# Grouped-query attention of a macaron encoder: head pairs between query tiles and out-projection units, on one core

## Chip, core and metric

The kernel runs on one core of a Trainium2 chip. The metric is the device time in microseconds of one execution. It is measured several times and the median counts.

## What is computed

The reference prepends 16 meta tokens to 256 frames (272 tokens, width 1024) and runs two layers. Each layer is a half-step SwiGLU block (hidden width 2816), a token mixer and another half-step SwiGLU block, each with an RMS norm before and after. The mixer of the first layer is stick-breaking attention, that of the second, which the change touches, is grouped-query attention with 16 heads of 64, four key and value heads, a window of two chunks of 64 frames, the 16 meta tokens always visible, rotary positions and a learned sink logit for each head:

```python
s_meta = einsum('bnqhgd,bmhd->bnhgqm', qf, k_meta) * scale
s_band = where(visible, einsum('bnqhgd,bnkhd->bnhgqk', qf, k_band) * scale, -inf)
p = softmax(concatenate([s_meta, s_band, sink], axis=-1), axis=-1)
o_frames = einsum(p_meta, v_meta) + einsum(p_band, v_band)
return o @ w_out
```

All is fp32. The meta rows of the output are dropped at the end, so in the last two sub-layers only frames are needed, except for the keys and values of the meta tokens.

## The kernel before

**Products.** Activations lie transposed, features on partitions and tokens in columns. Every weight product is made of three fp32r products, because weights and activations are each split into a high part (rounded to fp32r) and a low part: w_lo·y_hi + w_hi·y_hi + w_hi·y_lo (`three`, lines 1049 to 1054). Small products (scores, values, rotations, transposes, sums over partitions) are plain fp32, and the profile shows two records for each of them, except for a transpose, which has one.

**Weights.** They come in panels of 128 x 2048 (1 MB), numbered through all six sub-layers. SyncE loads them in this order into two raw slots (line 376), each load waiting for the low split two panels earlier. ScalarE casts a half of a panel into w_hi (`hi_half`, 427 to 435, cast at 435), VectorE subtracts for w_lo (`lo_half`, 661 to 667). There are four slots of w_hi and w_lo, and a slot is free when TensorE has signalled `panel_done` for the panel four earlier. An input panel has 256 output columns in two tiles of 128 (each 8 x 3 products), an output panel takes 256 input rows (8 output tiles x 2 x 3 products).

**The sub-layers** (`plan`, 117 to 124) are ffn, sb (stick-breaking), ffn, ffn, swa (grouped-query), ffn. On TensorE each begins with a head: the first three input panels are worked at the same time, k by k, at the pace in which VectorE and ScalarE deliver the normed input (1062 to 1105). Lines 1413 to 1431 are the sums of squares for the post-norm and four idle products that fill the wait for it. In sb the attention is written in head pairs and issued between its own input tiles and output columns by a written-out order of slots (`SB_AT`, `SB_HI`, `SB_LO`, lines 1248 to 1272); the two heads of a pair alternate on the two halves of TensorE's rows (scores, 1170 to 1181) or columns (values, 1221 to 1235).

**The swa sub-layer before.** Panels come in the order K, Q0 to Q3, V (`SWA_PANELS`). TensorE finishes all six (`in_panel`, 1107), with the rotations for rope (`rotate`, 1127, line 1136) between the last ones, and VectorE drains each panel with the norm's factor (line 768) and applies rope (`rope`, 752: sine product 756, sum 760; the cosine product is GpSimd's, line 410). ScalarE copies the keys into kd for both halves of the partitions (568), GpSimd copies the value windows (420).
Then comes the attention, head by head, in steps `st` (1335 to 1343): `scores(st)`, `turn(st - 8)`, `values(st - 9)`. Around it VectorE does `mask_scores` (scale and mask, line 880), `maxima` over two heads at a time (889), `sink_maxima` for four (899 to 903), `normalise` (910 to 918) and `save_o` (923); ScalarE does `exps(st - 5)` (575 to 580), the copy of the turned probabilities (593) and the high part of the output (584). Weight splits stand still in these steps. At the end TensorE does the four output panels (`out_panel`, 1390), the first of them waiting for all outputs.

## Time and profile before

| | |
|---|---|
| runs: median (lowest to highest) | 1082.48 us (1080.39 to 1085.07), 3 runs |
| the profiled execution's own time | 1080.6 us |
| its span, first to last instruction | 1078.8 us |
| TensorE busy | 1058.6 us, 98% |
| VectorE busy | 636.9 us, 59% |
| ScalarE busy | 508.8 us, 47% |
| mean granted TensorE clock | 0.995 |

Engines are called PE (TensorE), PEld (its weight loads, which overlap it), DVE (VectorE), ACT (ScalarE), POOL (GpSimd) and SP (SyncE). PEclk is the granted TensorE clock as a share of 2.4 GHz. A timeline row has the start, the length from the first start to the last end, the engine, the line, the names written and read, the shape, and how many records it merges; in brackets is the idle time in front of it and who ended it. Since products are pipelined, the end of one row lies behind the start of the next, and prices are best read from start to start.

### The profile page before, as it was taken

To read this page: it belongs to the slowest core of one execution; us is meant where nothing else is said; L and a number is where in the kernel's file an instruction comes from. 1 tells how busy PE (TensorE), PEld (TensorE's weight loads), DVE (VectorE), ACT (ScalarE), POOL (GpSimd) and SP (SyncE) were. 2 spreads that over 40 slices of the span, in tenths; PEclk is the share of its full clock that TensorE was granted. 3 is DMA by queue.
4 is the path that set the end of the run, shared out by engine and by line. 5 is a ranking of instruction groups with operands and counts; after the bars stand their busy time and mean duration, and the time that the engine had idled before them with its cause. 6 is when DMAs were issued, how large, how long until landed. Compare 5 with 4: busy or idle time off the path is not lost.

```text
span 1078.8 us, 19938 instructions
## 1 busy us (share of the span) xinstructions
PE 1058.6 (98%) x8082; PEld 1019.0 (94%) x8082; DVE 636.9 (59%) x840; ACT 508.8 (47%) x710; POOL 11.5 (1%) x20
## 2 busy tenths in 40 slices
PE   9999999999999999999999999999997999999997
PEld 8999999999899999999999999999995799999986
DVE  5765544576564776554457755534777667656443
ACT  5643433456454564343345543433544746544433
POOL 0000000000000000000000000000021000000000
PEclk9999999999999999999999999999998999999999
DMA  7564555413433265544542645545250053655551
GB/s 273 201 228 166 183 163 189 156 45 114 149 124 116 84 228 199 173 176 168 184 156 101 233 173 171 180 165 186 78 188 8 7 190 123 252 180 185 196 176 39
DMA packets 25828, 170.13 MB, mean 158 GB/s; under 512 B 3120, under 2 KB 3888, under 8 KB 5808
## 3 DMA queue, kind: packets, MB, share of 16 engines
q1 hardware_dynamic: 24624, 167.26, 43.9%
q10 hardware_dynamic: 1152, 2.11, 0.6%
q8 instruction: 41, 0.67, 0.2%
q14 instruction: 11, 0.09, 0.0%
HBM read 168.31 MB, written 1.05 MB: 157 GB/s over the span
## 4 chain that ended last, share of the span: by engine, by line
PE 93%; DVE 3%; ACT 1%; DMA 1%; issue 0%; SPq 0%; DVEq 0%; ACTq 0%
PE ps L1052 24%; PE ps L1053 24%; PE ps L1054 24%; PE ps L1087 3%; PE ps L1096 3%; PE ps L1089 3%; PE ps L1352 2%; PE ps L1353 2%; PE ps L1351 2%; PE ps L1211 1%; PE ps L1313 1%; DMA raw<-in_panels_dram 1%; PE ps L1299 1%; PE ps L1230 1%; PE ps L1423 1%; PE ps L1178 1%
## 5 line engine op out<-in xcount | busy, mean ns | idle before, releaser
L435 ACT CAST w_hi<-raw 128x1024 fp32r<-128x1024 f32 x310 | 310.2, 1048 | 404.2 <-PE ps L1054 313.1
L666 DVE TENSOR_TENSOR w_lo<-raw,w_hi 128x1024 fp32r<-128x1024 f32 x310 | 368.8, 1229 | 197.5 <-ACT w_hi L435 197.1
L1052 PE MATMUL ps<-y_hi,w_lo 128*128 128x272 f32 (+1 forms) x1522 | 440.1, 289 | 1.8 <-DVE y_lo L923 1.0
L1054 PE MATMUL ps<-y_lo,w_hi 128*128 128x272 f32 (+1 forms) x1522 | 437.3, 287 | 0.0
L1053 PE MATMUL ps<-y_hi,w_hi 128*128 128x272 f32 (+1 forms) x1522 | 435.6, 286 | 0.0
L1052 PEld LDWEIGHTS ps<-y_hi,w_lo 128*128 128x128 f32 x1522 | 286.7, 188 | 3.8 <-issue 2.9
L1053 PEld LDWEIGHTS ps<-y_hi,w_hi 128*128 128x128 f32 x1522 | 286.7, 188 | 0.3
L1054 PEld LDWEIGHTS ps<-y_lo,w_hi 128*128 128x128 f32 x1522 | 286.7, 188 | 0.0
L1053 PE MATMUL ps<-h_hi,w_hi 128*128 (+1 forms) x528 | 152.5, 289 | 0.0
L1054 PE MATMUL ps<-h_lo,w_hi 128*128 (+1 forms) x528 | 151.9, 288 | 0.0
L1052 PE MATMUL ps<-h_hi,w_lo 128*128 (+1 forms) x528 | 151.5, 287 | 0.0
L1054 PEld LDWEIGHTS ps<-h_lo,w_hi 128*128 128x128 f32 x528 | 99.5, 189 | 0.0
L1052 PEld LDWEIGHTS ps<-h_hi,w_lo 128*128 128x128 f32 x528 | 99.5, 188 | 0.0
L1053 PEld LDWEIGHTS ps<-h_hi,w_hi 128*128 128x128 f32 x528 | 99.4, 188 | 0.0
L741 DVE TENSOR_TENSOR hid<-act,ps 128x544 f32<-128x544 f32 (+1 forms) x44 | 31.2, 710 | 73.7 <-PE ps L1054 73.7
L736 DVE TENSOR_TENSOR act<-ps,rms_inv 128x544 f32<-128x544 f32 (+1 forms) x44 | 31.5, 716 | 58.8 <-PE ps L1054 55.1
L1087 PE MATMUL ps<-y_hi,w_lo 128*128 128x272 f32 (+1 forms) x238 | 61.7, 291 | 3.6 <-DVE y_hi L1036 2.7
L1089 PE MATMUL ps<-y_hi,w_hi 128*128 128x272 f32 (+1 forms) x238 | 60.8, 287 | 0.0
L1087 PEld LDWEIGHTS ps<-y_hi,w_lo 128*128 128x128 f32 x238 | 44.7, 188 | 6.2 <-DVE y_hi L1036 4.8
L1089 PEld LDWEIGHTS ps<-y_hi,w_hi 128*128 128x128 f32 x238 | 44.8, 188 | 0.0
L1096 PE MATMUL ps<-y_lo,w_hi 128*128 128x272 f32 (+1 forms) x238 | 36.5, 287 | 0.0
L1352 PE MATMUL ps<-w_hi,h_hi 128*128 128x512 f32 x88 | 34.8, 395 | 0.0
(134 smaller groups left out, 926.6 us busy)
## 6 DMA issues: line engine op xcount, KB each, us to landing
raw<-in_panels_dram SPq DMA_DIRECT2D x155, 1024.0 KB, 4.8
raw<-in_panels_dram SPq DMA_DIRECT2D x6, 256.0 KB, 8.8
sq<-in_panels_dram SPq DMA_DIRECT2D x1, 1024.0 KB, 10.0
out_dram<-fT SPq DMA_DIRECT2D x4, 256.0 KB, 2.0
const<-in_const_dram ACTq DMA_DIRECT2D x1, 920.0 KB, 4.7
xT<-in_x_dram ACTq DMA_DIRECT2D x3, 272.0 KB, 8.0
raw<-in_panels_dram SPq DMA_DIRECT2D x4, 128.0 KB, 3.8
gain_row<-in_row_dram SPq DMA_DIRECT2D x1, 512.0 KB, 5.5
```

What stands on the lines that cost most here:

```text
L435: nc.scalar.copy(w_hi[:, g % SLOTS, part], raw_part(g, part)).then_inc(hi_ready, 1)
L666: nc.vector.tensor_tensor(w_lo[:, g % SLOTS, part], raw_part(g, part), w_hi[:, g % SLOTS, part].bitcast(F32), ALU.subtract).then_inc(lo_re ...
L736: nc.vector.tensor_tensor(act[:, j % 2, :, t0:L], ps[:, b0:b0 + 2, t0:L], spread(rms_inv, 2, t0), ALU.mult).then_inc(gate_ready, 1)
L741: nc.vector.tensor_tensor(hid[:, j % 2, :, t0:L], act[:, j % 2, :, t0:L], ps[:, b0:b0 + 2, t0:L], ALU.mult).then_inc(h_ready, 1)
L1052: nc.tensor.matmul(dst, w_lo[:, slot, pc], yh, start=first, stop=False)
L1053: nc.tensor.matmul(dst, w_hi[:, slot, pc], yh, start=False, stop=False)
L1054: return nc.tensor.matmul(dst, w_hi[:, slot, pc], yl, start=False, stop=last)
L1087: nc.tensor.matmul(dst, w_lo[:, g % SLOTS, pc], y_hi[:, k, t0:L], start=(k == 0), stop=False)
L1089: nc.tensor.matmul(dst, w_hi[:, g % SLOTS, pc], y_hi[:, k, t0:L], start=False, stop=False)
L1096: nc.tensor.matmul(ps[:, BANK_IN[i][c], t0:L], w_hi[:, g % SLOTS, pc], y_lo[:, k, t0:L], start=False, stop=False)
L1351: nc.tensor.matmul(dst, hh[:, cols], w_lo[:, slot, at:at + 512], start=first, stop=False)
L1352: nc.tensor.matmul(dst, hh[:, cols], w_hi[:, slot, at:at + 512], start=False, stop=False)
```

## The change

The panels come as K, V, Q0 to Q3. The head works K, V and Q0; the other six query tiles are issued one in each slot, at 256 columns. The attention runs in head pairs, twelve slots in all, with the 16 units of the out-projection (12 products each) from slot 6 on. Weight splits are spread over the slots by halves. The key copy kd becomes kx, the keys with the two partition halves exchanged. Mask, scale and maximum become one operation, `tensor_tensor_reduce`, which writes s = -(score*scale + mask), since op is `(in0 + in1) * scale` with scale -1/8 and the mask is 0 or -1e30, and the running minimum that starts at minus the sink. Exponentials and normalisation go by pairs. The outputs have buffers of their own (sw_hi, sw_lo). The core of the diff:

```diff
-SWA_PANELS = [4, 0, 1, 2, 3, 5]
-SW_EXP, SW_LAG = 5, 8
+SWA_PANELS = [4, 5, 0, 1, 2, 3]
+SW_K, SW_V, SW_Q = 0, 2, 4
+SW_TILES, SW_SLOTS = 6, 12
+SW_HI = [1] * 10 + [2, 2, 2]
+SW_LO = [2] + [1] * 9 + [2, 2, 3]
+SW_OUT = [(6, 0), (6, 1), (7, 0), (7, 1), (5, 0), (5, 1), (0, 0), (1, 0)]
+SW_FILL = {6: ([(0, 0)], [(0, 1)]), 7: ([(0, 2)], []), 8: ([(1, 0)], [(1, 1)]), 9: ([(1, 2)], [(0, 3)]),
+           10: ([(1, 3)], [(2, 0)]), 11: ([(2, 1)], [(2, 2), (2, 3)])}
```

ScalarE's order:

```diff
+                    for st in range(SW_SLOTS + 1):
+                        if 0 <= st - 4 < PAIRS:
+                            save_p(st - 4)
+                        hi_halves(2 + sum(SW_HI[:st]), SW_HI[st])
...
+                        if 0 <= st - 2 < PAIRS:
+                            exps(st - 2)
+                        if 0 <= st - 4 < PAIRS:
+                            o_high(st - 4)
```

VectorE's new operation and its order:

```diff
+                    def logits(p):
+                        for half in range(2):
+                            h = 2 * p + half
+                            v.wait_ge(s_done, p + 1)
+                            if p >= 3:
+                                v.wait_ge(pt_done, 2 * (p - 3) + half + 1)
                             for c in range(2):
                                 k0, k1 = SW_COL[c], SW_COL[c] + SW_KEYS[c]
+                                nc.vector.tensor_tensor_reduce(
+                                    out=s[:, p % 3, half, k0:k1], in0=ps[:, half, k0:k1], in1=cst("mask_sw", P, k0, k1),
+                                    scale=-SCALE, scalar=neg_sinks[:, h:h + 1], op0=ALU.add, op1=ALU.min,
+                                    accum_out=neg[:, p % 3, half, c:c + 1]).then_inc(neg_ready, 1)
...
+                    for st in range(SW_SLOTS + 1):
+                        n0 = sum(SW_LO[:st])
+                        if 0 <= st - 3 < PAIRS:
+                            normalise(st - 3)
+                        lo_halves(n0, 1)
+                        if st < SW_TILES:
+                            drain_tile(st)
+                        if st == 0:
+                            rope(0)
+                            rope(1)
+                        elif st in (2, 4, 6):
+                            rope(st // 2 + 1)
+                        if 0 <= st - 1 < PAIRS:
+                            logits(st - 1)
+                        if 0 <= st - 4 < PAIRS:
+                            o_low(st - 4)
+                        lo_halves(n0 + 1, SW_LO[st] - 1)
```

TensorE's blocks and their order:

```diff
+                    def scores(p):
+                        kv = p // 2
+                        pe.wait_ge(roped, 2 + p // 2)
+                        if p == 0:
+                            pe.wait_ge(kx_ready, 2)
+                        if p >= 1:
+                            pe.wait_ge(neg_ready, 4 * p)
+                        for at, tok, n in SW_RUNS:
+                            q0 = META if at == 0 else META + P
+                            for half in range(2):
+                                r = slice(HD * half, HD * half + HD)
+                                keys = qkv[r, SW_K + kv // 2] if half == kv % 2 else kx[r, kv // 2]
+                                mm = nc.tensor.matmul(ps[:, half, at:at + n], qkv[r, SW_Q + p, q0:q0 + P],
+                                                      keys[:, tok:tok + n], start=True, stop=True,
+                                                      skip_group_check=True)
                         mm.then_inc(s_done, 1)
...
+                    def values(p):
+                        vc = slice(HD * (p // 2), HD * (p // 2) + HD)
+                        pe.wait_ge(pt_saved, 2 * p + 2)
+                        if p >= 1:
+                            pe.wait_ge(ol_ready, 8 + p)
                         for n, (c, _, zero) in enumerate(SW_WIN):
+                            for half in range(2):
+                                r = slice(HD * half, HD * half + HD)
+                                mm = nc.tensor.matmul(ps[r, 4, P * c:P * c + P], vt[:, n, vc],
+                                                      p_t[:, p % 2, half, P * n:P * n + P], start=(zero == 0),
+                                                      stop=(zero > 0), skip_group_check=True)
+                        mm.then_inc(sw_o, 1)
...
+                    def out_unit(j, n):
+                        g = t.g_out + j
+                        pe.wait_ge(lo_ready, 2 * g + 2)
+                        pe.wait_ge(ol_ready, 8 + 2 * j + 2)
...
+                    for st in range(SW_SLOTS):
+                        if st < SW_TILES:
+                            in_tile(st)
+                        for unit in SW_FILL.get(st, ([], []))[0]:
+                            out_unit(*unit)
+                        if st == 0:
+                            rotate(0)
+                            rotate(1)
+                        elif st in (2, 4, 6):
+                            rotate(st // 2 + 1)
+                        if 0 <= st - 1 < PAIRS:
+                            scores(st - 1)
+                        if st == 1:
+                            turn_v()
+                        if 0 <= st - 4 < PAIRS:
+                            values(st - 4)
+                        for unit in SW_FILL.get(st, ([], []))[1]:
+                            out_unit(*unit)
+                        if 0 <= st - 3 < PAIRS:
+                            turn(st - 3)
+                    for n in range(4):
+                        out_unit(3, n)
```

GpSimd keeps its five cosine products, now into two alternating buffers (rot_c), and does the value windows (two fills and five copies) after the second one. PSUM banks: scores 0 and 1, turned probabilities 2 and 3, outputs of a pair 4, rotations 5, tiles 6 and 7; the first out units take 6, 7, 5 and at last 0 and 1 in half banks (SW_OUT).

## Rows read from the trace of the kernel before

**Rows 1.** The page, busy time by engine (share of the span, instructions)

```profile
PE 1058.6 (98%) x8082; PEld 1019.0 (94%) x8082; DVE 636.9 (59%) x840; ACT 508.8 (47%) x710; POOL 11.5 (1%) x20
```

**Rows 2.** Windows: stretch, busy by engine, PEclk, DMA share, GB/s

```profile
240.00:340.00 100.00, 99.07 (x802) 91.40 (x801) 60.54 (x81) 52.79 (x64) 0.00 (x0) 1.00 0.33 117
818.40:828.60 10.20, 7.75 (x33) 5.40 (x31) 8.52 (x27) 5.41 (x21) 1.34 (x1) 0.50 0.00 1
```

**Rows 3.** Timeline of TensorE in the grouped-query sub-layer: start us, length us, what

```profile
794.62 1.16 PE L1136 MATMUL ps<-qkv,const 128*128 128x272 f32 x4 [1.32 <-DVE qkv L768]
...
803.30 0.49 PE L1052 MATMUL ps<-y_hi,w_lo 128*128 128x272 f32 x1
...
809.55 1.99 PE L1136 MATMUL ps<-qkv,const 128*128 128x272 f32 x8
811.47 3.28 PE L1284 MATMUL ps<-kd,qkv 64*128 64x144 f32 x28
...
817.86 1.38 PE L1326 MATMUL ps<-const,v_win 128*128 128x128 f32 x8 [3.11 <-DVE rot_s L756]
...
823.17 1.12 PE L1299 MATMUL ps<-const,s 128*128 128x128 f32 x4 [2.45 <-DVE s L918]
...
831.05 0.86 PE L1284 MATMUL ps<-kd,qkv 64*128 64x144 f32 x4
831.84 0.65 PE L1299 MATMUL ps<-const,s 128*128 128x128 f32 x4
832.42 1.09 PE L1313 MATMUL ps<-p_t,vt 128*64 128x128 f32 x8
833.44 0.86 PE L1284 MATMUL ps<-kd,qkv 64*128 64x144 f32 x4
...
858.21 0.35 PE L1052 MATMUL ps<-y_hi,w_lo 128*128 128x256 f32 x1 [1.01 <-DVE y_lo L923]
...
880.84 1.74 PE L1423 MATMUL ps<-sq,const 128*128 128x256 f32 x6
```

**Rows 4.** Timeline of TensorE in the stick-breaking attention

```profile
275.21 1.14 PE L1230 MATMUL ps<-fT,v_tok 128*64 128x272 f32 x12 [0.93 <-ACT fT L525]
276.28 0.41 PE L1203 MATMUL ps<-sp,const 128*128 128x32 f32 x2
...
289.38 1.20 PE L1178 MATMUL ps<-qkv 64*128 64x16 f32 x12
290.51 0.39 PE L1052 MATMUL ps<-y_hi,w_lo 128*128 128x272 f32 x1
...
293.73 1.20 PE L1178 MATMUL ps<-qkv 64*128 64x16 f32 x12
```

**Rows 5.** Timeline of VectorE, the grouped-query sub-layer

```profile
781.37 2.36 DVE L666 TENSOR_TENSOR w_lo<-raw,w_hi 128x1024 fp32r<-128x1024 f32 x2
...
812.45 1.39 DVE L880 SCALAR_TENSOR_TENSOR s<-ps,const 128x352 f32<-128x352 f32 x3 [1.91 <-PE ps L1284]
813.75 0.94 DVE L889 TENSOR_REDUCE top<-s 128x2 f32<-128x288 f32 x2
...
820.23 0.71 DVE L756 TENSOR_TENSOR rot_s<-ps,const 128x544 f32<-128x544 f32 x1
...
821.74 0.52 DVE L880 SCALAR_TENSOR_TENSOR s<-ps,const 128x352 f32<-128x352 f32 x1
...
822.58 0.98 DVE L918 TENSOR_SCALAR s<-s,inv 128x144 f32<-128x144 f32 x4
```

**Rows 6.** Timeline of ScalarE, the same stretch

```profile
834.93 0.58 ACT L593 COPY p_t<-ps 128x512 f32<-128x512 f32 x1 [0.70 <-PE ps L1299]
...
836.17 0.19 ACT L578 ACTIVATION_READ_ACCUMULATOR s<-s,neg 128x1 f32 x1
...
857.50 3.90 ACT L435 CAST w_hi<-raw 128x1024 fp32r<-128x1024 f32 x4
```

**Rows 7.** The page, DMA issues: KB each, median us to landing

```profile
raw<-in_panels_dram SPq DMA_DIRECT2D x155, 1024.0 KB, 4.8
```

More of the change, by code:

```diff
@@ L139, in bank_post, with out_tile, out_pair, first_col @@
     return bank_out(t)[2]
-ROT_BANK = [4, 6, 4, 6, 4]
-ROPE_AT = {4: 3, 6: 4}
+def out_tile(ps, t, d):
+    if t.kind == "swa":
+        bank, half = SW_OUT[d]
+        return ps[:, bank, 256 * half:256 * half + 256]
+    return ps[:, bank_out(t)[d], t.t_out:L]
+def out_pair(ps, t, n):
+    if t.kind == "swa" and n < 3:
+        return ps[:, SW_OUT[2 * n][0], :].rearrange("p (a n) -> p a n", a=2)
+    if t.kind == "swa":
+        return ps[:, 0:2, 0:256]
+    b0 = bank_out(t)[2 * n]
+    return ps[:, b0:b0 + 2, t.t_out:L]
+def first_col(t, i):
+    return META if t.kind == "swa" and i >= 2 else t.t_in
 HEAD = 3
@@ L339, in build @@
         pairs_before = [11 * sum(1 for t in SUBS[:u] if t.kind == "ffn") for u in range(7)]
-        drained_before = [sum(t.n_in for t in SUBS[:u] if t.kind == "swa") for u in range(7)]
         def steps(eng, n, body):
@@ new lines, in rope @@
+                    def rope(b):
+                        c0 = 0 if b == 0 else META
+                        row = SW_K if b == 0 else SW_Q + 2 * b - 2
+                        turned = ps[:, 0:2, 0:L] if b == 0 else ps[:, 5, :].rearrange("p (a n) -> p a n", a=2)
+                        v.wait_ge(rot_done, b + 1)
+                        nc.vector.tensor_tensor(rot_s[:, :, c0:L], turned, spread(cst("sin"), 2, c0),
+                                                ALU.mult).then_inc(rs_ready, 1)
+                        v.wait_ge(rs_ready, b + 1)
+                        v.wait_ge(rc_ready, b + 1)
+                        nc.vector.tensor_tensor(qkv[:, row:row + 2, c0:L], rot_s[:, :, c0:L],
+                                                rot_c[:, b % 2, :, c0:L], ALU.add).then_inc(roped, 1)
+                        v.wait_ge(roped, b + 1)
@@ new lines, in o_low @@
+                    def o_low(p):
+                        v.wait_ge(oh_ready, 8 + p + 1)
+                        nc.vector.tensor_tensor(sw_lo[:, p, :], ps[:, 4, 0:SEQ], sw_hi[:, p, :].bitcast(F32),
+                                                ALU.subtract).then_inc(ol_ready, 1)
+                    for i in range(3):
+                        drain_head(i)
+                    v.wait_ge(sinks_landed, 16)
+                    nc.vector.tensor_scalar(neg_sinks[:], sinks[:], -1.0, None, ALU.mult).then_inc(sinks_ready, 1)
@@ L1048, in _, with three @@
         def _(pe):
-            def three(dst, slot, col, yh, yl, first, last):
+            def three(dst, slot, col, yh, yl, first, last, shared=False):
                 pc = slice(col, col + P)
-                nc.tensor.matmul(dst, w_lo[:, slot, pc], yh, start=first, stop=False)
-                nc.tensor.matmul(dst, w_hi[:, slot, pc], yh, start=False, stop=False)
-                return nc.tensor.matmul(dst, w_hi[:, slot, pc], yl, start=False, stop=last)
+                nc.tensor.matmul(dst, w_lo[:, slot, pc], yh, start=first, stop=False, skip_group_check=shared)
+                nc.tensor.matmul(dst, w_hi[:, slot, pc], yh, start=False, stop=False, skip_group_check=shared)
+                return nc.tensor.matmul(dst, w_hi[:, slot, pc], yl, start=False, stop=last, skip_group_check=shared)
             for t in SUBS:
@@ new lines, in turn @@
+                    def turn(p):
+                        for half in range(2):
+                            h = 2 * p + half
+                            pe.wait_ge(p_ready, 2 * h + 2)
+                            if p == 0:
+                                pe.wait_ge(v_saved_a, half + 1)
+                            else:
+                                pe.wait_ge(pt_saved, h - 1)
+                            for n, (c, k0, _) in enumerate(SW_WIN):
+                                at = SW_COL[c] + k0
+                                mm = nc.tensor.transpose(ps[:, 2 + half, P * n:P * n + P],
+                                                         s[:, p % 3, half, at:at + P], cst("ident"))
+                            mm.then_inc(pt_done, 1)
```

413 lines of the change are left out of this document (160 added, 253 removed).

## Prediction

> **What bounds the kernel now.** I read the page first: TensorE is busy for 98% of the span, VectorE for 59% and ScalarE for 47% [rows 1]. So only TensorE's own work, its few idle stretches and its clock are worth anything. The windows show where the clock fails: the whole stick-breaking attention runs at granted clock 1.00, but 818.4 to 828.6 us, the front of the grouped-query attention, at 0.50 [rows 2], the lower of the two levels (1.2 instead of 2.4 GHz), with 7.75 us of 10.2 busy. TensorE had just been idle for 3.11 us there.
>
> TensorE's timeline from 793 to 881 us [rows 3] shows the rest. The first query panel ends at 794.62 − 1.32 = 793.30; a panel takes 809.55 − 803.30 = 6.25 us, so the stretch that the change rewrites begins at 787.05 (the end of the head that is paced by the norm) and ends at 880.84, where the post-norm sums begin: **93.8 us**. In it TensorE is idle for 1.32 (VectorE drains late, between weight splits), 3.11 (the value transposes wait for a rope), 2.45 (first probabilities) and 1.01 us (last output's low part): 7.9 us. In the steady part one head costs 831.84 − 831.05 = 0.79 for scores, 0.58 for four transposes, 833.44 − 832.42 = 1.02 for values.
>
> **The change, part by part, on TensorE.** All prices are start to start.
>
> - Query tiles. Four query panels take only the 256 frame columns, no longer 272. The out-projection has that width: (880.84 − 858.21) / 192 products = 0.1179 us each [rows 3]. Six tiles of 24 products are left (the third head panel lies before 787.05): 16.98 us. A tile between blocks of another kind pays for the change-over: one at 272 columns took 293.73 − 290.51 = 3.22 us [rows 4], times 256/272 = 3.03. I take 6 × 3.03 = 18.2. The head's third panel saves 48 × 0.0074 = 0.35 before 787.05 (0.0074 is 16/256 of 0.1179).
> - Rotations. Four full products in 811.47 − 809.55 = 1.92 [rows 3]: 0.48 each. Two of 272 and eight of 256 columns: 4.6.
> - Scores. Now both heads of a pair are issued turn about, on the two halves of the array's rows. Rows 3 have this by accident: seven heads in a row, odd and even, took 3.28 us, 0.94 a pair, against 2 × 0.79. The stick-breaking scores, already written in pairs, took 290.51 − 289.38 = 1.13 for 432 columns [rows 4]; for 352, 0.92. I take 0.96: 8 × 0.96 = 7.7.
> - Transposes: as before, 64 of them, 16 × 0.58 = 9.3. Value transposes once, 1.3 (8 of them, 1.38 long [rows 3]).
> - Values. A pair's products alternate between two halves of the array's columns. The stick-breaking values do just that: 276.28 − 275.21 = 1.07 for a pair with 544 columns each [rows 4], where the same columns one after the other would take twice that by the pace of rows 3 (512 columns in 1.02). With 512: 1.01, I take 1.02: 8.2, where 16 × 1.02 = 16.3 were.
> - Out-projection: 192 products at 0.1179 = 22.6, as before, but 12 of 16 units now stand between attention blocks. With about ten change-overs at (3.22 − 24 × 0.1179 × 272/256) = 0.21 at most, I take 1.8: 24.4.
>
> Sum: 18.2 + 4.6 + 7.7 + 9.3 + 1.3 + 8.2 + 24.4 = **73.7**, so 93.8 − 73.7 = 20.1, plus 0.35 is 20.4 us. The old 7.9 us of idling and the slow stretch are within the 93.8 and so within this gain, if nothing takes their place. A page speaks against the interleaving: TensorEngine Tiling (Array Packing) in the Trainium skill, section "Key Properties", says that a change of tiling mode drains the array. The trace prices this at no more than the 0.21 above; and the pairs halve the number of changes inside attention.
>
> **Do the other engines keep up?** One slot of TensorE, in the middle (tile 3.03, rotation 0.9 in every second, scores 0.96, values 1.02, transposes 1.17): 7.1 or 6.2 us. From slot 6 on units (1.6) take the tile's place; slot 7 is the shortest: 4.75.
> - VectorE [rows 5]: normalising a pair 1.4 (from 0.43 after 821.74 to 822.58 + 0.98), one weight split 1.18 (2.36 for two), a tile's drain about 0.4 (rope's 0.71 is for twice the width), rope 1.5 in every second slot (820.23 to 821.74), o_low 0.4, and the logits. Without the logits 4.9 or 3.4.
> - The new logits operation is in no row. Four a pair, of 144 and 208 columns. Below: no dearer than the plain one it resembles, 0.43 for 352 columns (three in 1.30), so 1.0 a pair with four starts. Above: as dear as the old operation and the old maximum one after the other, 2 × 0.43 + 0.94 = 1.8 a pair. It is one pass like the first, so I take 1.3. That makes 6.2 or 4.7 us on VectorE against 7.1 or 6.2: hidden. In slot 7 it is 4.7 against 4.75.
> - ScalarE [rows 6]: a save and one head's exponentials 836.36 − 834.93 = 1.43, twice, one conversion 0.98 (3.90 for four), o_high and the sinks 0.6: 4.4 us. Hidden. kx is two copies in slot 0, where twelve copies for kd were.
> - GpSimd: five cosine products as before, and seven copies and fills in the place of six. All its work in the kernel is 11.5 us [rows 1]; the part that the value transposes need, two products and the copies, is about half of that and starts at 787, so it ends by 793, before slot 1 asks at 795.7. rot_c now alternates between two buffers, so rope waits for it less.
> - DMA: SP's loads are in the same order; each waits for the split two panels earlier and lands 4.8 us later [rows 7]. Splits now come one half a slot, so loads spread over the attention, where rows 2 show the queue idle. Only the first output panel comes late (by the walk its load starts at about 795, ScalarE could cast it at 797) and holds the first exponentials back to about 803, and the first normalisation starts there anyway.
>
> Walking the slots with these prices, three places are tight. The first out unit (slot 6) follows o_low of pair 1 by 0.4 us; unit (1,0) in slot 8 meets o_low of pair 3 with nothing to spare; and where a scores block follows a logits group the semaphore hop counts. I give these 1.2 us together: below, 0; above, with logits at 1.8 a pair, about 3, since o_low stands behind the logits on VectorE. The last panel's units follow the last o_low by 1.7 us, and ScalarE has two conversions (1.95) left when they start, released by the third panel's end as now, so the post-norm is as before.
>
> Net: 20.4 − 1.2 = **19.2 us**. The profiled execution took 1080.6 us, so 1061.4; the median of the runs is 1.9 above it, so 1063.3. I forecast 1063 us, with TensorE at granted clock 1.00 through the stage, since the denser stick-breaking stage shows that for the same mix [rows 2].
>
> **Rivals.**
> - A: chained slots. VectorE and ScalarE serve tiles, ropes, logits, outputs and splits in one fixed order, so one late operation delays a drain, a load, then a tile. The widths above are for average slots; if 1 us is lost in six of the eight middle slots, 6 of 19 us are given back: 1069. For: slot 7 has no margin. Against: in most slots VectorE has 1 to 1.5 us to spare. Chance 0.13.
> - A2: the logits operation streams at half the pace of the old one: 4 × 0.43 = 1.7 a pair, with four starts 2.1 [rows 5]. That is 0.8 more in each slot; most of it is absorbed where VectorE waits for the scores anyway, but o_low is pushed past the first out units, 2 to 4 us lost: 1066. Chance 0.03. A page would have it so: the Vector Engine (DVE) Microarchitecture Reference in the Trainium skill, section "Points that are easy to get wrong", says that an operation of this accumulating family with two non-bf16 SBUF sources has half throughput. Here one source lies in PSUM, and no run so far shows it.
> - B: pairs do not overlap, as with two heads' values one after the other. Then scores cost 8 × 0.64 and values 8 × 1.02 more, 13.3: 1076.5. Against: rows 4 have both shapes. 0.05.
> - C, slower: the new logits operation is far dearer. Then VectorE sets the slot: slots 1 to 8 would take 4.2 + 4t each (t for one operation), the rest 27 us, which equals 93.8 at t = 1.04, against 0.3 taken. Already at t = 1.4 it is 8 × 9.8 + 27 = 105.4, 11.6 us more than now: 1094. Against: the old maximum, a reduction too, took 0.94 for a pair's 704 columns [rows 5]. 0.03.
> - D: only a third of the gain arrives, by A and B together: 1078 to 1085. 0.03.
>
> **Numbers.** The forecast itself has 0.73 (A 0.13, A2 0.03, B 0.05, C 0.03, D 0.03). What a measurement of this kernel can tell from no change is about 0.5%, 5.4 us. Faster 0.94, same 0.03, slower 0.03. Range: below, no new waits and no change-over cost, 1.2 + 3 less, 1059; above, A's 1069 and a margin for the runs' own scatter (1080.4 to 1085.1), 1070.
>
> **What would show it.** TensorE from the end of the head to the post-norm sums: about 75 us. Scores of a pair below 1.1 and values below 1.1. No idle of more than 0.5 us, least of all before the value transposes. No clock at 0.50 in the stage. Logits: 16 × 2 operations of about 0.3 us and a reading of the accumulator, if it has a record of its own. If the idle on TensorE behind VectorE adds up to over 3 us, A is right. If a pair takes the sum of two heads, B. The forecast is wrong above 1070.

## Result, and the profile after

| | before | after |
|---|---|---|
| median (lowest to highest), 4 executions each | 1082.67 us (1080.39 to 1085.07) | 1056.49 us (1056.02 to 1056.70) |
| the profiled execution's own time / span | 1080.6 / 1078.8 us | 1056.58 / 1054.8 us |
| mean granted clock of that execution | 0.995 | 0.999 |

The ratio is 0.9768, 95% interval 0.9754 to 0.9782: 2.3% faster. Between the two profiled executions the difference is 24.0 us, between the medians 26.2. The forecast, 1063 us with a range from 1059 to 1070, had the sign and the mechanism and gave too little: 19.2 us of gain in the profile where 24.0 came, and a range that ends 2.5 us above the measured time.

The page of the changed kernel, the two lines that answer to [rows 1] and the span:

```profile
span 1054.8 us, 20040 instructions
...
PE 1042.6 (99%) x8114; PEld 1007.8 (96%) x8114; DVE 629.9 (60%) x864; ACT 508.1 (48%) x712; POOL 10.9 (1%) x21
```

TensorE is now idle for 12 us in all, before for 20. The window over the rewritten stretch (stretch, busy PE, PEld, DVE, ACT, POOL, PEclk, DMA share, GB/s) answers to [rows 2]:

```profile
786.00:857.00 71.00, 70.91 (x658) 64.78 (x656) 58.01 (x161) 50.25 (x133) 9.47 (x12) 1.00 0.36 129
```

TensorE is busy for 70.91 of 71.00 us and the clock is at 1.00 throughout: nothing is left of the 0.50 stretch. TensorE's timeline, to be set against [rows 3] (L1281 and L1284 rotations, L1301 scores, L1339 value transposes, L1316 transposes, L1328 values, L1059 the first product of a tile or unit, L1462 the post-norm sums):

```profile
789.10 1.08 PE L1281 MATMUL ps<-qkv,const 128*128 128x272 f32 x4
...
794.77 1.09 PE L1339 MATMUL ps<-const,v_win 128*128 128x128 f32 x8
795.62 0.36 PE L1059 MATMUL ps<-y_hi,w_lo 128*128 128x256 f32 x1
...
798.54 1.02 PE L1284 MATMUL ps<-qkv,const 128*128 128x256 f32 x4
799.50 0.39 PE L1301 MATMUL ps<-qkv 64*128 64x144 f32 x1
...
800.49 0.39 PE L1059 MATMUL ps<-y_hi,w_lo 128*128 128x256 f32 x1
...
810.21 1.09 PE L1328 MATMUL ps<-p_t,vt 128*64 128x128 f32 x16
811.23 1.09 PE L1316 MATMUL ps<-const,s 128*128 128x128 f32 x8
812.08 0.36 PE L1059 MATMUL ps<-y_hi,w_lo 128*128 128x256 f32 x1
...
817.08 1.09 PE L1316 MATMUL ps<-const,s 128*128 128x128 f32 x8
818.12 0.35 PE L1059 MATMUL ps<-sw_hi,w_lo 128*128 128x256 f32 x1
...
824.11 1.04 PE L1316 MATMUL ps<-const,s 128*128 128x128 f32 x8
824.90 0.36 PE L1059 MATMUL ps<-sw_hi,w_lo 128*128 128x256 f32 x1
...
828.51 1.09 PE L1316 MATMUL ps<-const,s 128*128 128x128 f32 x8
829.69 0.36 PE L1059 MATMUL ps<-sw_hi,w_lo 128*128 128x256 f32 x1
...
856.68 1.74 PE L1462 MATMUL ps<-sq,const 128*128 128x256 f32 x6
```

One slot can be read in it: the tile from 795.62, the rotation 0.96 from 798.54, a pair's scores 0.99 from 799.50, the next tile from 800.49. A pair's values take 811.23 − 810.21 = 1.02 and its eight transposes 812.08 − 811.23 = 0.85, or 0.79 at 824.11, where a unit stands ahead of them instead of the values; a weight product follows in both cases. They are longer only where TensorE waits behind them: 1.04 at 817.08, in front of unit (0,0), and 1.18 at 828.51, in front of unit (1,0). These are two of the three places that the forecast called tight; the third, scores behind a logits group, shows no wait.

VectorE (the new operation is L907, its accumulator has a record of its own):

```profile
796.11 0.36 DVE L907 CUSTOM_DVE_ANT_0 s<-ps,const,neg_sinks 128x144 f32<-128x144 f32 x1
796.40 0.08 DVE L907 DVE_READ_ACCUMULATOR2_ANT neg<- 128x1 f32 x1
796.40 0.43 DVE L907 CUSTOM_DVE_ANT_0 s<-ps,const,neg_sinks 128x208 f32<-128x208 f32 x1
...
797.40 0.08 DVE L907 DVE_READ_ACCUMULATOR2_ANT neg<- 128x1 f32 x1
...
827.60 0.37 DVE L907 CUSTOM_DVE_ANT_0 s<-ps,const,neg_sinks 128x144 f32<-128x144 f32 x1 [1.33 <-PE ps L1301]
...
829.12 0.42 DVE L928 TENSOR_TENSOR sw_lo<-ps,sw_hi 128x256 fp32r<-128x256 f32 x1
```

From 796.11 to 797.40 the four operations of a pair take 1.29 us, as taken in the sum (1.3). In slot 7 the scores come late for VectorE (it waits 1.33), so o_low of pair 3 starts at 829.12, and unit (1,0) starts 0.57 later.

### The profile page after: what moved, and what is told of

It reads as the page before. It is cut to its first block, busy times and chain, and to the rows that moved or that the text cites. A ratio compares the mean times of both kernels' runs of the same rounds, so it can differ in the third digit from the quotient of the medians.

```text
span 1054.8 us, 20040 instructions
## 1 busy us (share of the span) xinstructions
PE 1042.6 (99%) x8114; PEld 1007.8 (96%) x8114; DVE 629.9 (60%) x864; ACT 508.1 (48%) x712; POOL 10.9 (1%) x21
## 4 chain that ended last, share of the span: by engine, by line
PE 95%; DVE 1%; DMA 1%; ACT 1%; issue 0%; SPq 0%; DVEq 0%; ACTq 0%
PE ps L1059 25%; PE ps L1060 25%; PE ps L1061 25%; PE ps L1095 3%; PE ps L1104 3%; PE ps L1097 3%; PE ps L1395 2%; PE ps L1396 2%; PE ps L1394 2%; PE ps L1197 1%; DMA raw<-in_panels_dram 1%; PE ps L1216 1%; PE ps L1462 1%; PE ps L1328 1%; PE ps L1301 1%; PE ps L1164 1%
## 5 line engine op out<-in xcount | busy, mean ns | idle before, releaser
L1059 PE MATMUL ps<-y_hi,w_lo 128*128 128x272 f32 (+1 forms) x1458 | 421.7, 289 | 0.8 <-DVE pre_ms L722 0.6
L1061 PE MATMUL ps<-y_lo,w_hi 128*128 128x272 f32 (+1 forms) x1458 | 418.9, 287 | 0.0
L1060 PE MATMUL ps<-y_hi,w_hi 128*128 128x272 f32 (+1 forms) x1458 | 417.4, 286 | 0.0
L1059 PEld LDWEIGHTS ps<-y_hi,w_lo 128*128 128x128 f32 x1458 | 274.7, 188 | 2.7 <-issue 1.9
L1060 PEld LDWEIGHTS ps<-y_hi,w_hi 128*128 128x128 f32 x1458 | 274.6, 188 | 0.2
L1061 PEld LDWEIGHTS ps<-y_lo,w_hi 128*128 128x128 f32 x1458 | 274.7, 188 | 0.0
L1059 PE MATMUL ps<-h_hi,w_lo 128*128 (+1 forms) x528 | 151.5, 287 | 0.0
L1059 PEld LDWEIGHTS ps<-h_hi,w_lo 128*128 128x128 f32 x528 | 99.5, 188 | 0.0
L1095 PE MATMUL ps<-y_hi,w_lo 128*128 128x272 f32 (+1 forms) x238 | 61.5, 290 | 3.8 <-DVE y_hi L1043 2.7
L1097 PE MATMUL ps<-y_hi,w_hi 128*128 128x272 f32 (+1 forms) x238 | 60.6, 286 | 0.0
L1095 PEld LDWEIGHTS ps<-y_hi,w_lo 128*128 128x128 f32 x238 | 44.8, 188 | 6.3 <-DVE y_hi L1043 4.8
L1097 PEld LDWEIGHTS ps<-y_hi,w_hi 128*128 128x128 f32 x238 | 44.8, 188 | 0.0
L1104 PE MATMUL ps<-y_lo,w_hi 128*128 128x272 f32 (+1 forms) x238 | 36.5, 287 | 0.0
```

What stands on the lines that cost most here:

```text
L1059: nc.tensor.matmul(dst, w_lo[:, slot, pc], yh, start=first, stop=False, skip_group_check=shared)
L1060: nc.tensor.matmul(dst, w_hi[:, slot, pc], yh, start=False, stop=False, skip_group_check=shared)
L1061: return nc.tensor.matmul(dst, w_hi[:, slot, pc], yl, start=False, stop=last, skip_group_check=shared)
L1095: nc.tensor.matmul(dst, w_lo[:, g % SLOTS, pc], y_hi[:, k, c0:L], start=(k == 0), stop=False)
L1097: nc.tensor.matmul(dst, w_hi[:, g % SLOTS, pc], y_hi[:, k, c0:L], start=False, stop=False)
L1104: nc.tensor.matmul(ps[:, BANK_IN[i][c], c0:L], w_hi[:, g % SLOTS, pc], y_lo[:, k, c0:L], start=False, stop=False)
```

## Experiments

Eleven runs were made: nine variants, and each of the two kernels once more. Those of one group ran on one chip, beside the kernel before; its median there was 1080.57 us (28 executions) for the first four, 1080.12 (9) for the next four, 1081.78 (9) for the last three. The changed kernel itself ran first and in the last group (1056.49 and 1056.92), so differences of the middle ones from it are good to about half a microsecond.

### Why the old kernel scatters: the clock

The first kernel is the kernel before, unchanged.

> The kernel before, once more, to see why its executions scatter by 4.7 us (1080.4 to 1085.1) where those of the changed kernel scatter by 0.7. Theory (clock): each execution loses more or less to a lowered granted clock in the attention, so the longer executions show a lower mean clock; 0.995 goes with about 1080.5, and 1085 should go with about 0.990. Rival (memory or start-up): the mean clock is the same, 0.995, in long and short executions, and the extra time lies outside the attention.

Its twelve executions, each with its mean granted clock, and those of the kernel before that ran beside it:

| mean clock | e0, us | before, same chip, us |
|---|---|---|
| 0.993 to 0.997 | 1079.38, 1079.65, 1080.53, 1080.92 | 1078.76 to 1082.18 (19) |
| 0.991 | 1081.94 to 1082.96 (6) | 1082.11 to 1082.86 (6) |
| 0.989 | 1084.59, 1085.47 | 1084.02, 1084.33, 1084.59 |

The clock theory holds: with one exception (1082.18 at 0.995) the clock alone sorts all 40 executions into these three groups of times. A mean of 0.991 over 1080 us is some 19 us at half clock by estimate, where the profiled execution has 10.2 in the attention and a little at the very end.

The second kernel gives TensorE something to do in the two idle stretches:

```diff
+                    def fill(bank, count):
+                        for _ in range(count):
+                            nc.tensor.matmul(ps[:, bank, 0:160], cst("ones"), cst("sin", P, 0, 160),
+                                             start=True, stop=True, skip_group_check=True)
                     def turn_v():
+                        pe.wait_ge(s_ready, 4)
+                        fill(3, 9)
                         pe.wait_ge(win_ready, 4)
...
+                        if st == SW_LAG:
+                            pe.wait_ge(rs_ready, 5)
+                            fill(5, 7)
                         if 0 <= st - SW_LAG < NH:
                             turn(st - SW_LAG)
```

> The kernel before with sixteen small fp32 products more, whose results are not used, issued into its two idle stretches (nine ahead of the value transposes, seven ahead of the first probabilities). Theory (clock): the granted clock stays at 1.00 through the attention; the 5.4 us after the second stretch that ran at the lower level shrink by 2.7, the idling itself stays: 1078 to 1080 us, and the executions scatter by less than 1.5 us. Rival (the clock has another cause than the idling): the 0.50 stretch stays and the time is 1082 to 1084, with the old scatter.

Measured: 1077.53 us, 1077.18 to 1078.23 in eleven executions, every one at 0.999 or 1.000. Its timeline (L1320 are the fillers), and the window over the attention:

```profile
814.34 2.71 PE L1320 MATMUL ps<-const 128*128 128x160 f32 x18 [0.42 <-DVE s L880]
...
820.16 2.17 PE L1320 MATMUL ps<-const 128*128 128x160 f32 x14 [1.27 <-DVE rot_s L756]
```

```profile
811.00:855.00 44.00, 40.80 (x297) 32.12 (x294) 32.30 (x104) 27.23 (x95) 2.67 (x3) 1.00 0.00 1
```

Most of the two idle stretches is now filled with work of no use: what is left of them is 0.42 us ahead of the first fillers and 1.27 ahead of the second. The attention ran at 1.00 and the time fell by 3.0 us against the median beside it, to half a microsecond below the range that was expected, and by more against the executions at 0.991. The scatter went from 6 us to 1. So the idling, not the attention's kind of work, brings the clock down, and the loss differs from one execution to the next. The clock did not fall behind the short stretches that are left in any execution. Why the low level lasts once 10 us and once 20 stays open.

### Pairs without interleaving

The kernel before with TensorE's order changed alone:

```diff
-                    for st in range(NH + SW_LAG + 1):
-                        if st < NH:
-                            scores(st)
+                    for st in range(0, NH + SW_LAG + 2, 2):
+                        for h in (st, st + 1):
+                            if h < NH:
+                                scores(h)
                         if st == 6:
                             turn_v()
-                        if 0 <= st - SW_LAG < NH:
-                            turn(st - SW_LAG)
-                        if st - SW_LAG >= 1:
-                            values(st - SW_LAG - 1)
+                        if st - SW_LAG >= 2:
+                            values_pair((st - SW_LAG) // 2 - 1)
+                        for h in (st - SW_LAG, st - SW_LAG + 1):
+                            if 0 <= h < NH:
+                                turn(h)
```

values_pair alternates between the halves as the changed kernel does.

> The kernel before, with TensorE alone reordered: scores, values and transposes by head pairs, values alternating between the halves, nothing put in between and the other engines' orders as they were. Theory (the pairs save work, the interleaving hides the chain): TensorE's work falls by about 17 us, but VectorE's 3.6 and ScalarE's 3.1 us a pair now exceed TensorE's 2.8, so only 6 to 10 us arrive: 1073 to 1077, with idle TensorE behind VectorE or ScalarE at each pair. Rival (the pairs alone are the gain): 1064 to 1067.

Measured: 1077.08 us (1075.96 to 1077.87), 3.5 us less than the kernel before beside it, where 6 to 10 were expected. TensorE's busy time falls by 10 us, from 1058.6 to 1048.2, and its idle time grows by 7, from 20 to 28. What is new in it is the wait of the values for ScalarE's copies of the turned probabilities, 8.5 us in seven waits. Four rows of TensorE's timeline (L1299 transposes, L1345 values, L1284 scores) and two of ScalarE's (L578 an exponential, L593 the copy):

```profile
832.59 1.09 PE L1299 MATMUL ps<-const,s 128*128 128x128 f32 x8
833.61 0.87 PE L1284 MATMUL ps<-kd,qkv 64*128 64x144 f32 x8
...
839.04 1.09 PE L1345 MATMUL ps<-p_t,vt 128*64 128x128 f32 x16 [1.56 <-ACT p_t L593]
...
842.73 1.09 PE L1345 MATMUL ps<-p_t,vt 128*64 128x128 f32 x16 [1.57 <-ACT p_t L593]
```

```profile
841.24 0.42 ACT L578 ACTIVATE s<-s,neg 128x144 f32<-128x144 f32 x1
...
842.10 0.57 ACT L593 COPY p_t<-ps 128x512 f32<-128x512 f32 x1
```

A pair has a period of 3.7 us (839.04 to 842.73), of which TensorE stands still for 1.56. Scores, transposes and values of the changed kernel need 2.9 us a pair. About 0.9 us of the wait (841.24 to 842.10) is ScalarE at another head's exponentials between the two copies of a pair, since its order still goes head by head here, while the changed kernel makes both copies one after the other.

The clock is low where it was low in the kernel before, behind two early idle stretches (here 1.83 and 2.55 us, there 3.11 and 2.45), and not behind the waits of 1.56 us:

```profile
819.00:829.00 10.00, 7.45 (x43) 5.74 (x43) 9.62 (x30) 4.83 (x19) 1.08 (x1) 0.50 0.00 1
838.00:848.00 10.00, 5.83 (x69) 4.84 (x70) 7.30 (x28) 8.26 (x32) 0.00 (x0) 1.00 0.00 0
```

So the pairs save work, and with the other engines' orders as they were most of it is lost again in waits. How much of the rest is owed to the interleaving and how much to ScalarE's order by pairs stays open: no run has the pairs with that order and nothing between them.

### What one block costs

Values of a pair head after head:

```diff
-                        for n, (c, _, zero) in enumerate(SW_WIN):
-                            for half in range(2):
+                        for half in range(2):
+                            for n, (c, _, zero) in enumerate(SW_WIN):
```

> The changed kernel with the value products of a pair issued head after head instead of alternating. Theory (the two halves of the array's columns work at the same time): a pair takes 1.85 to 2.0 us instead of 1.03, all of it on TensorE's path: 8 x 0.9 = 7 us more, 1063 to 1065. Rival (no overlap, the price was saved by leaving out change-overs): at most 1 us more, 1057.

Measured: 1060.37 us (1059.99 to 1060.85), 3.9 more than the changed kernel, half of what was expected:

```profile
809.99 1.58 PE L1328 MATMUL ps<-p_t,vt 128*64 128x128 f32 x16
811.50 1.09 PE L1316 MATMUL ps<-const,s 128*128 128x128 f32 x8
```

A pair takes 1.51, not 2.0: 8 × (1.51 − 1.02) = 3.9. The edit does not take the overlap away, it only shortens it. The single starts in the trace show this: the first head's eight records start from 809.99 to 810.81, some 0.11 us apart, and the second head's from 810.49 to 811.30, so the second head begins when half of the first is issued. In the middle both are under way, and eight records are in progress within a quarter of a microsecond, against five where the second head is alone:

```profile
810.65:810.90 0.25, 0.25 (x8) 0.25 (x6) 0.25 (x1) 0.00 (x0) 0.00 (x0) 1.00 0.00 0
811.05:811.30 0.25, 0.25 (x5) 0.25 (x3) 0.21 (x2) 0.00 (x0) 0.00 (x0) 1.00 0.84 229
```

Issued alternately, the second head starts 0.007 us behind the first, and the pair takes 1.02, as long as one head alone in the kernel before (833.44 − 832.42 = 1.02 [rows 3]). So on the values the overlap is complete, and 3.9 us is what half of it is worth. The price of a pair without any overlap was measured in no run.

Scores head after head, the same edit with the loops over `half` and `SW_RUNS` exchanged:

```diff
-                        for at, tok, n in SW_RUNS:
-                            q0 = META if at == 0 else META + P
-                            for half in range(2):
+                        for half in range(2):
+                            for at, tok, n in SW_RUNS:
+                                q0 = META if at == 0 else META + P
```

> The changed kernel with the score products of a pair issued head after head instead of alternating. Theory (the two halves of the array's rows overlap only while both heads have products in flight): a pair takes 1.4 to 1.6 us instead of 0.99, 8 x 0.5 = 4 us more: 1060 to 1061.5. Rival (no overlap to lose): below 1057.5.

Measured: 1059.05 us (1058.38 to 1059.49), 2.6 more, less than both ends of the expectation and clear of the rival:

```profile
800.23 0.53 PE L1301 MATMUL ps<-qkv 64*128 64x144 f32 x3
800.58 0.39 PE L1301 MATMUL ps<-kx,qkv 64*128 64x144 f32 x1
...
800.96 0.32 PE L1301 MATMUL ps<-qkv 64*128 64x192 f32 x1
...
801.57 0.38 PE L1059 MATMUL ps<-y_hi,w_lo 128*128 128x256 f32 x1
```

1.34 a pair against 0.99, 8 × 0.35 = 2.8. Here too the heads still overlap: the second (the rows with kx) begins at 800.58, while the last record of the first starts at 800.96.

The transposes of a pair apart: `turn(p, halves)` issues the first head's before the values and the second's after the unit.

```diff
+                        if 0 <= st - 3 < PAIRS and st >= 4:
+                            turn(st - 3, (0,))
                         if 0 <= st - 4 < PAIRS:
                             values(st - 4)
                         for unit in SW_FILL.get(st, ([], []))[1]:
                             out_unit(*unit)
                         if 0 <= st - 3 < PAIRS:
-                            turn(st - 3)
+                            turn(st - 3, (1,) if st >= 4 else (0, 1))
```

> The changed kernel with the two heads' transposes of a pair no longer next to each other: the first head's stand ahead of the value products, the second's after the out unit. Theory (the step that I mis-sized: four transposes alone cost 0.58 because 0.2 of it is change-over, eight in a row cost 0.8): TensorE has one block more in seven slots, 7 x 0.2 = 1.4 us more, and perhaps a wait or two since the first head's probabilities are wanted earlier: 1057.5 to 1059. Rival (the transposes are cheaper for another reason, full clock or neighbours): within 0.5 us of 1056.5.

Measured: 1058.27 us (1058.09 to 1058.93), 1.4 to 1.8 more, the time that the theory gave. The profiles do not bear out its account. From the second pair of scores to the post-norm sums this kernel takes 58.5 us and the changed one 57.2 (856.68 − 799.50). Of the 1.4 between them 0.8 are longer waits ahead of units (0,0) and (1,0), since less stands between the values and the unit. Only 0.6 is work in the seven slots: 0.14 to 0.17 more in a slot where the first block stands behind scores, and nothing in the two where it stands behind a unit. That the total is 1.4 was luck.

What the block behind the transposes costs can be read from two blocks of four, both behind a unit:

```profile
826.32 0.60 PE L1316 MATMUL ps<-const,s 128*128 128x128 f32 x4
826.67 0.36 PE L1059 MATMUL ps<-sw_hi,w_lo 128*128 128x256 f32 x1
...
839.43 0.60 PE L1316 MATMUL ps<-const,s 128*128 128x128 f32 x4
839.95 1.09 PE L1328 MATMUL ps<-p_t,vt 128*64 128x128 f32 x16
```

In front of values (full array to half arrays) four cost 0.52, in front of a weight product (full array again) 0.35, so 0.17 of the old 0.58 a head was the change to the values behind it. About half of this comes back elsewhere: the first weight product behind transposes takes 0.20 to its successor instead of 0.12. Standing behind scores instead of a unit costs another 0.06 (four cost 0.59 there, at 823.19).

Tiles of 272 columns instead of 256:

```diff
-    return META if t.kind == "swa" and i >= 2 else t.t_in
+    return t.t_in
...
-                            mm = three(ps[:, 6 + c, META:L], g % SLOTS, 256 * k + P * c, y_hi[:, k, META:L],
-                                       y_lo[:, k, META:L], k == 0, k == KT - 1)
+                            mm = three(ps[:, 6 + c, 0:L], g % SLOTS, 256 * k + P * c, y_hi[:, k, 0:L],
+                                       y_lo[:, k, 0:L], k == 0, k == KT - 1)
```

> The changed kernel with all query panels at 272 columns again, as before, instead of the 256 frame columns. Theory: 4 x 48 products of 0.0074 us more each, all on TensorE's path, 1.4 us more than the changed kernel beside it. Rival (start to start is not set by the columns at this width): no difference.

Measured: 1058.29 us (1057.82 to 1058.43) against 1056.92 beside it, 1.4 more, as expected.

### What VectorE had to spare

The fused operation undone: for each head of a pair `scalar_tensor_tensor` with scale −1/8 and the mask subtracted, two `tensor_reduce` with min, and a min with the sink.

```diff
-                                nc.vector.tensor_tensor_reduce(
-                                    out=s[:, p % 3, half, k0:k1], in0=ps[:, half, k0:k1], in1=cst("mask_sw", P, k0, k1),
-                                    scale=-SCALE, scalar=neg_sinks[:, h:h + 1], op0=ALU.add, op1=ALU.min,
-                                    accum_out=neg[:, p % 3, half, c:c + 1]).then_inc(neg_ready, 1)
+                            nc.vector.scalar_tensor_tensor(out=s[:, p % 3, half], in0=ps[:, half, 0:SW_W],
+                                                           scalar=-SCALE, in1=cst("mask_sw"), op0=ALU.mult,
+                                                           op1=ALU.subtract).then_inc(masked, 1)
...
+                                nc.vector.tensor_reduce(low[:, half, c:c + 1], s[:, p % 3, half, k0:k1],
+                                                        AX.X, ALU.min).then_inc(lowest, 1)
...
+                            nc.vector.tensor_tensor(neg[:, p % 3, half, :], low[:, half, :],
+                                                    neg_sinks[:, h:h + 1].broadcast_to([P, 2]),
+                                                    ALU.min).then_inc(neg_ready, 2)
```

> The changed kernel with mask and maximum as separate operations again: in a pair two masking operations, four minima and two small ones, in the place of the four fused ones that take 1.29 us. Theory (VectorE has 1 to 1.5 us to spare in most slots, and the first two out units wait for o_low): VectorE takes about 1 us more a pair, 0.5 to 2 us arrive: 1057 to 1058.5. Rival (VectorE is close behind TensorE, so the fused operation is what makes the interleaving work): 1062 or more.

Measured: 1059.85 us, between the two: two executions at clock 0.999 took 1058.62 and 1059.04, two at 0.997 took 1060.66 and 1061.06. The profiled one is of the second kind:

```profile
816.72 1.09 PE L1329 MATMUL ps<-const,s 128*128 128x128 f32 x8
819.84 0.36 PE L1072 MATMUL ps<-sw_hi,w_lo 128*128 128x256 f32 x1 [2.03 <-issue]
...
821.33 1.89 PE L1297 MATMUL ps<-qkv,const 128*128 128x256 f32 x4
823.15 0.61 PE L1314 MATMUL ps<-qkv 64*128 64x144 f32 x1
```

```profile
820.00:830.00 10.00, 10.00 (x78) 8.52 (x79) 8.32 (x24) 3.79 (x13) 0.00 (x0) 0.83 0.30 105
```

Unit (0,0) now starts after 2.03 us of idling, behind the transposes of 816.72; the row names no releaser ("issue"), but VectorE's timeline shows it:

```profile
817.23 0.94 DVE L908 SCALAR_TENSOR_TENSOR s<-ps,const 128x352 f32<-128x352 f32 x2
818.09 1.05 DVE L916 TENSOR_REDUCE low<-s 128x1 f32<-128x144 f32 x4
...
819.33 0.42 DVE L941 TENSOR_TENSOR sw_lo<-ps,sw_hi 128x256 fp32r<-128x256 f32 x1
```

The mask (817.23), the minima (818.09) and the min with the sink stand ahead of o_low (819.33), and the unit starts 0.51 behind it. Behind this wait the clock falls: the four rotation products take 823.15 − 821.33 = 1.82 us to the next block (the changed kernel: 799.50 − 798.54 = 0.96), and the window shows 0.83 over 10 us. So the slower VectorE costs 2.1 to 2.6 us in the executions at 0.999, and the idling that it opens costs another 2 in those at 0.997; only one of the latter was profiled. The fused operation is not what most of the gain is made of, but it keeps the first out unit on time.

### A try at more

The two waits that are left, and four changes of kind, might go with another order of the units. The first step moves (0,0) and (1,0) behind the values:

```diff
-SW_FILL = {6: ([(0, 0)], [(0, 1)]), 7: ([(0, 2)], []), 8: ([(1, 0)], [(1, 1)]), 9: ([(1, 2)], [(0, 3)]),
+SW_FILL = {6: ([], [(0, 0), (0, 1)]), 7: ([(0, 2)], []), 8: ([], [(1, 0), (1, 1)]), 9: ([(1, 2)], [(0, 3)]),
```

> The changed kernel with the out units of slots 6 and 8 moved: both stand behind the values, none at the front of the slot. Theory (the two waits ahead of units (0,0) and (1,0), 0.2 and 0.35 us, come from o_low being just in time; and two change-overs go): 0.5 to 1.0 us less, 1055.5 to 1056. Rival (a new wait: values stand only 1.0 us behind the transposes of the slot before, and ScalarE's two copies take that long): 0 to 1 us more.

Measured: 1056.21 us (1055.21 to 1056.90), not told apart from the changed kernel by its times. In the profile the rewritten part is shorter: from the scores of pair 4 (815.89, slot 5) to the last six units (848.38) it takes 32.5 us, in the changed kernel's second profile (814.97 to 847.93) 33.0, the low end of what was expected. The second step also puts both units of slots 9 and 10 at the front, and ran beside the changed kernel itself:

```diff
-SW_FILL = {6: ([(0, 0)], [(0, 1)]), 7: ([(0, 2)], []), 8: ([(1, 0)], [(1, 1)]), 9: ([(1, 2)], [(0, 3)]),
-           10: ([(1, 3)], [(2, 0)]), 11: ([(2, 1)], [(2, 2), (2, 3)])}
+SW_FILL = {6: ([], [(0, 0), (0, 1)]), 7: ([(0, 2)], []), 8: ([], [(1, 0), (1, 1)]), 9: ([(1, 2), (0, 3)], []),
+           10: ([(1, 3), (2, 0)], []), 11: ([(2, 1)], [(2, 2), (2, 3)])}
```

> The changed kernel once more, beside its variants on the same chip. Theory (clock): at a mean clock of 0.999 or 1.000 in each execution, its times stay within 1.5 us of each other while those of the kernel before on this chip fall into groups by clock: 1079 to 1081 at 0.995 to 0.997, 1082 to 1083 at 0.991, above 1084 at 0.989. Median 1056 to 1057.

> The changed kernel with out units joined wherever no wait follows: slots 6 and 8 behind the values, slots 9 and 10 both at the front of the slot, so that TensorE changes its kind of work four times less and the two small waits in front of units (0,0) and (1,0) go. Theory: 0.55 from the waits and 0.1 to 0.2 for each change-over, 0.8 to 1.2 us less than the changed kernel beside it. Rival (the blocks between hid a copy of ScalarE's, which now shows): no gain or a loss.

Measured: the changed kernel again 1056.92 us (1055.71 to 1056.96), every execution at 0.998 or above, beside the kernel before in its three groups (1078.79 to 1081.18 at 0.995 to 0.996, 1081.78 to 1083.05 at 0.991, 1084.34 at 0.989). The variant 1057.00 (1056.67 to 1057.87): no gain, the rival. Last six units and post-norm sums, the variant first, then the changed kernel:

```profile
847.43 0.38 PE L1059 MATMUL ps<-sw_hi,w_lo 128*128 128x256 f32 x1
...
856.99 1.95 PE L1462 MATMUL ps<-sq,const 128*128 128x256 f32 x6 [0.64 <-ACT sq L674]
```

```profile
847.93 0.39 PE L1059 MATMUL ps<-sw_hi,w_lo 128*128 128x256 f32 x1
...
856.54 1.74 PE L1462 MATMUL ps<-sq,const 128*128 128x256 f32 x6
```

The attention does end 0.5 us earlier (847.43 against 847.93), but the last six units take 8.92 + 0.64 us instead of 8.61, since ScalarE is late with the squares (the wait of 0.64 for sq). Its last weight halves wait for a load and start at 852.14, in the changed kernel at 851.25, and the load waits for a split that VectorE starts 1.0 us later (844.83, 843.87), behind the output of a pair whose values came later. The 0.5 us moved into the next wait. No version that beats the changed kernel was found.

## Why the prediction fell short

The stretch began at 789.10 − 2.98 = 786.12 (the first tile at the mean of the others) and ended at 856.68: 70.6 us, where the steps gave 73.7 of work and 1.2 of waits.

| step | forecast | measured |
|---|---|---|
| six tiles | 18.2 | 17.9 |
| rotations | 4.6 | 4.5 |
| scores | 7.7 | 8.0 |
| transposes of pairs | 9.3 | 6.5 |
| value transposes | 1.3 | 0.85 |
| values | 8.2 | 8.2 |
| out-projection | 24.4 | 24.1 |
| new waits | 1.2 | 0.6 |

**The step that failed** is "Transposes: as before, 64 of them, 16 × 0.58". The 0.58 was read start to start in a kernel that changed its kind of work after every four and went on to values each time, so it held the price of these changes along with the work. Eight in a row in front of a weight product cost 0.79 to 0.85 in the changed kernel, so 64 cost 6.5 us and not 9.3. That is 2.8 of the 4.3 us. Two things make it up. Two heads' transposes in one block save 0.14 a pair: in e2, between values and scores, eight cost 833.61 − 832.59 = 1.02 instead of 2 × 0.58, 1.1 us in all. Weight products behind them, and in half of the slots ahead of them too, save another 0.17 to 0.23 a pair, 1.7 us; e6 shows the 0.17 in blocks of four. The value transposes (1.3 in the sum, 0.85 now) were priced in [rows 3] from a row at 817.86, where the clock was falling: 0.45 us too much.

**The second is the carry to the median**, "the median of the runs is 1.9 above it, so 1063.3". e0 and e1 show that this 1.9 is time at half clock in the old kernel's worse executions; it goes with the idling and must not be carried over. On the profiled execution's own time, 1061.4, the forecast was 4.8 off instead of 6.5. The remaining half microsecond is the head (18.1 us instead of 18.6, 0.35 foreseen) and the start-up: from one execution to the next this sub-layer begins up to 1.4 us apart (767.5 to 768.9 us in the profiles).

**The range** had these two on one side only: below the forecast it allowed for no waits and no change-overs of tiles and units, and not for change-overs inside the old prices.

**Right**: TensorE is the bound in nearly every slot; the pairs overlap on the two halves; the clock stays at 1.00; logits at 1.3 a pair; two of the three tight places, though their waits add up to half of the 1.2; the change-overs of the out units (1.5 us over 192 × 0.1179, 1.8 taken); 1.4 us for the columns (e7). The 7.9 us of old idling leave out a fifth stretch of 0.41 us at 846.71; nothing in the sum rests on it.

**Rivals.**

- A (chained slots, 6 us back): not in the changed kernel, where 0.6 is lost. In e5, with a dearer logits step, a wait of this kind did come.
- A2 (half pace): wrong. An operation of 144 columns takes 796.40 − 796.11 = 0.29 us start to start, a pair of 144 and 208 (1.29 / 2) 0.645, so the one of 208 takes 0.355 and 64 columns more cost 0.065, 1.0 ns a column; the old one had 352 columns in 0.43 with its start, 1.2 ns a column at most, and half its pace would be about 2. The Vector Engine (DVE) Microarchitecture Reference in the Trainium skill, "Points that are easy to get wrong", has half throughput for two such sources in SBUF; here one lies in PSUM, and 1.0 ns a column is no half pace. The profile lists the operation under a name of its own (CUSTOM_DVE_ANT_0), so that it is one of those the page speaks of is not shown either.
- B (no overlap): wrong, since a pair's values cost what one head's did. Its price of 13.3 us is not tested: e3 and e4 cost 3.9 and 2.8 us, but the heads still overlap in them.
- C, D: nothing of them.

The forecast set change-overs against the change for tiles and units only. The old attention went from transposes to values once for every head, sixteen times, and the changed one never does, so in the transposes the change-overs were in its favour. TensorEngine Tiling (Array Packing), section "Key Properties", of the Trainium skill says that a change of tiling mode drains the array; the rows of e6 agree with it, but no run here tells the drain from another cause of the same 0.17 us.

## What to carry to other kernels

A start-to-start price includes the change to whatever follows: before it is multiplied into an order with other neighbours, look for the same block ahead of another kind, or a longer one. When executions scatter, sort them by mean clock before the scatter is added to a forecast, for an order that closes the idling takes the scatter along. Pairing heads on half arrays alone saved 3.5 us, since the chain of turning, copying and multiplying, with ScalarE's order by heads, did not keep up. When an overlap is to be priced by undoing it, look at the single starts first: in e3 and e4 the reordered products still overlapped in part.

## What was not expected of the hardware

The granted clock falls behind idle stretches of 1.8 to 3.1 us (e2, e5 and the kernel before), not in all executions and not for the same time: behind 2.03 us in e5 it was low for about 3.4 us (0.83 over 10 us) in the profiled execution and, by their mean of 0.999, hardly or not at all in two others, while in the old kernel the mean of 0.989 to 0.997 stands for about 6 to 24 us at half clock. It stayed at 1.00 in e2, where TensorE was idle for 1.56 us in every 3.7. Two plain fp32 values blocks on different halves of the array take 1.02 us issued alternately, no longer than one alone. Issued one behind the other they take 1.51, since the second starts when half of the first is issued. The fused operation has a second record for its accumulator, 0.08 us, that costs nothing beside the next one.
